# GpSimd takes over sums of squares and residual additions, and some weight splits are held back

## The reference, cut to what matters

```python
def rms_norm(x, w):
    xf = x.astype(jnp.float32)
    y = xf * lax.rsqrt(jnp.mean(xf * xf, -1, keepdims=True) + RMS_EPS)
    return (y * w.astype(jnp.float32)).astype(x.dtype)
...
    for i in range(DEPTH):                       # first block, DEPTH = 2
        a_in = rms_norm(hs, norm_w[i, 0])
        mix = gated_deltanet(a_in, ...) if i % N_MIXERS == 0 else mlstm(a_in, ...)
        hs = hs + keep * rms_norm(mix, norm_w[i, 1])                     # post-norm, residual
        f = conv_ffn(rms_norm(hs, norm_w[i, 2]), ffn_w_up[i], ..., ffn_w_down[i])
        hs = hs + keep * rms_norm(f, norm_w[i, 3])                       # post-norm, residual
...
    x = x + 0.5 * swiglu(rmsnorm(x, ffn1_norm), ffn1_w_gu, ffn1_w_down)  # second block
    z = rmsnorm(x, mix_norm) @ w_in
    ...
    x = x + merged @ w_out
    x = x + 0.5 * swiglu(rmsnorm(x, ffn2_norm), ffn2_w_gu, ffn2_w_down)
```

## Time and profile before

| | |
|---|---|
| median of 3 runs | 1910.94 us (1909.84 to 1913.47) |
| the profiled execution, its own time | 1910.32 us |
| its span | 1908.6 us |
| TensorE busy (matmul / weight load) | 1705.0 / 1614.5 us |
| VectorE, ScalarE, GpSimd busy | 1094.9, 832.7, 281.5 us |
| mean granted TensorE clock | 0.941 |

### The profile page before, as it was taken

One profiled execution on the slowest core, in us unless ns is written; L12 is line 12 of the kernel. 1 busy time (PEld: TensorE's weight loads), 2 busy tenths in 40 slices (PEclk: granted clock), 3 DMA queues, 4 the chain that ended last, 5 costly groups with the idle time before them and its releaser, 6 DMA issues.

```text
span 1908.6 us, 32571 instructions
## 1 busy us (share of the span) xinstructions
PE 1705.0 (89%) x13057; PEld 1614.5 (85%) x13057; DVE 1094.9 (57%) x1433; ACT 832.7 (44%) x1226; POOL 281.5 (15%) x343
## 2 busy tenths in 40 slices
PE   5986888889879999897579999799999989889998
PEld 4975888879869999795369999799998579889998
DVE  4862655556458864533458864555556376565654
ACT  5651233244446644542246654344443234644332
POOL 0000443410003320000003330122000000111120
PEclk8996799999989999895789999899999999999999
DMA  5540110115425444450025546354463343355543
GB/s 212 179 155 20 48 43 6 45 35 196 148 89 176 169 139 165 156 176 22 12 89 178 176 140 202 120 196 166 162 207 124 111 177 122 112 187 173 179 156 131
DMA packets 41566, 252.81 MB, mean 132 GB/s; under 512 B 4524, under 2 KB 6688, under 8 KB 19472
## 3 DMA queue, kind: packets, MB, share of 16 engines
q1 hardware_dynamic: 37376, 233.13, 35.7%
q0 software_dynamic: 4112, 18.61, 3.1%
HBM read 250.55 MB, written 1.17 MB: 132 GB/s over the span
## 4 chain that ended last, share of the span: by engine, by line
PE 77%; DVE 12%; ACT 6%; issue 3%; DMA 1%; POOL 1%; DVEq 0%; SPq 0%; ACTq 0%; POOLq 0%
PE bank L393 19%; PE bank L394 19%; PE bank L395 19%; ACT w_hi L281 3%; DVE w_lo L284 2%; PE bank L1088 2%; PE bank L397 2%; PE bank L563 2%; PE bank L1096 2%; PE bank L1099 2%; DVE rs L516 1%; PE bank L502 1%; DVE a L522 1%; DVE mix L522 1%; PE bank L1370 1%
## 5 line engine op out<-in xcount | busy, mean ns | idle before, releaser
L393 PE MATMUL bank<-work_r,w_hi 128*128 128x272 f32 (+1 forms) x3312 | 950.5, 287 | 63.3 <-DVE work_r L452 38.7
L394 PE MATMUL bank<-work_r,w_hi 128*128 128x272 f32 (+1 forms) x3312 | 944.3, 285 | 0.0
L395 PE MATMUL bank<-work_r,w_lo 128*128 128x272 f32 (+1 forms) x3312 | 943.5, 285 | 0.0
L284 DVE TENSOR_TENSOR w_lo<-ring,w_hi 128x2048 fp32r<-128x2048 f32 (+2 forms) x233 | 487.8, 2095 | 470.9 <-ACT w_hi L281 470.7
L393 PEld LDWEIGHTS bank<-work_r,w_hi 128*128 128x128 f32 x3312 | 632.1, 191 | 69.8 <-issue 38.2
L394 PEld LDWEIGHTS bank<-work_r,w_hi 128*128 128x128 f32 x3312 | 630.9, 190 | 0.4
L395 PEld LDWEIGHTS bank<-work_r,w_lo 128*128 128x128 f32 x3312 | 630.8, 190 | 0.0
L281 ACT ACTIVATE w_hi<-ring 128x2048 fp32r<-128x2048 f32 (+2 forms) x233 | 408.1, 1753 | 388.9 <-PE bank L395 388.8
L1248 DVE SCALAR_TENSOR_TENSOR work<-work,params_sb 128x272 f32<-128x272 f32 x176 | 122.7, 736 | 5.9
L1258 POOL TENSOR_TENSOR work<-work 128x272 f32<-128x272 f32 x44 | 44.9, 1020 | 344.6 <-ACT work L1232 344.6
L502 PE MATMUL bank<-sq,consts_sb 128*128 128x272 f32 (+1 forms) x170 | 48.7, 443 | 25.6 <-ACT sq L482 14.3
(11 more groups left out here) (387 smaller groups left out, 1881.7 us busy)
## 6 DMA issues: line engine op xcount, KB each, us to landing
ring<-in_stream SPq DMA_DIRECT2D x166, 1024.0 KB, 4.9
ring<-in_stream SPq DMA_DIRECT2D x64, 704.0 KB, 4.0
ring<-in_stream SPq DMA_DIRECT2D x10, 768.0 KB, 4.2
work<-rows_scratch POOLq DMA_DIRECT2D x4, 1632.0 KB, 8.0
work<-rows_scratch POOLq DMA_DIRECT2D x4, 544.0 KB, 9.1
work<-rows_scratch_o POOLq DMA_DIRECT2D x1, 2176.0 KB, 9.0
ring<-in_stream SPq DMA_DIRECT2D x3, 512.0 KB, 7.1
work<-rows_scratch_m POOLq DMA_DIRECT2D x1, 1088.0 KB, 7.1
```

What stands on the lines that cost most here:

```text
L284: eng.tensor_tensor(w_lo[:, slot, 0:size], raw_w, w_hi[:, slot, 0:size].bitcast(F32), ALU.subtract).then_inc(lo_done, 1)
L393: pe.matmul(out, w_hi[:, slot, at:at + P], hi, start=first, stop=False)
L394: pe.matmul(out, w_hi[:, slot, at:at + P], lo, start=False, stop=False)
L395: mm = pe.matmul(out, w_lo[:, slot, at:at + P], hi, start=False, stop=last)
```

## The change

Six sums of squares are shortened on TensorE: the four post-norms and the sums of in_uv and up3. GpSimd adds the squares of blocks 1 to 6 onto block 0 as they appear (`square_sums_pool`), and TensorE sums only that and block 7 (`norm_pooled_pe`). The residual additions of the four post-norms go from VectorE to GpSimd (`residual_pool`). At the four ends of the first block the split of the second slab of the next phase is held (`end="hold"`) and made by `prepare` later: on ScalarE behind the root of the post-norm, on VectorE behind the multiplications. ScalarE's square-root table is loaded at the start of the evacuations and not before the two roots that follow. `up2` has a lead of one slab where it had two; `up_dve` evacuates its first products before it splits, and in_uv's ScalarE splits before its first activation.

```diff
@@ each_product @@
+                body_first = split_last or begin == "body" and j == 0
+                if body_first:
                     body(Unit(ph, size, j, i, per_turn_))
-                if split:
+                if split and not (begin == "split" and per_turn_ == 0 and j == ph.parts - 1):
                     lo, hi = j * size * ph.per_product, (j + 1) * size * ph.per_product
                     slabs = range(lo // ph.parts, hi // ph.parts)
+                    if begin == "split" and j == 0:
+                        ahead(0, None)
                     for slab in slabs if end is None else slabs[:-1]:
                         ahead(slab, None if per_turn_ == 0 else i)
-                if not split_last:
+                if not body_first:
                     body(Unit(ph, size, j, i, per_turn_))
@@ new functions @@
+        def square_sums_pool(pool, turn, kind, use, n):
+            S.begin("square_sums")
+            for k in range(1, DB - 1):
+                pool.wait_ge(*S.at(f"{kind}_act", f"sq{k}", use))
+                if k > 1:
+                    S.own(pool, "square_sums", turn)
+                S.inc(pool.tensor_tensor(sq[:, 0, 0:n], sq[:, 0, 0:n], sq[:, k, 0:n], ALU.add), "square_sums")
+
+        def norm_pooled_pe(pe, turn, kind, use, n):
+            S.begin(f"{kind}_pe")
+            pe.wait_ge(*S.at("square_sums", turn=turn))
+            pe.matmul(stat[kind][:, 0:n], ones, sq[:, 0, 0:n], start=True, stop=False)
+            pe.wait_ge(*S.at(f"{kind}_act", f"sq{DB - 1}", use))
+            S.inc(pe.matmul(stat[kind][:, 0:n], ones, sq[:, DB - 1, 0:n], start=False, stop=True), f"{kind}_pe", "sums")
@@ norm_dve @@
-                if add is not None and 1 <= k <= blocks:
-                    dve.wait_ge(*S.at(f"{kind}_dve", f"k{k - 1}", use))
-                    S.inc(dve.tensor_tensor(add[1](k - 1), add[1](k - 1), dst(k - 1), ALU.add), "norm_add", k - 1)
+        def residual_pool(pool, use):
+            S.begin("norm_add")
+            for k in range(DB):
+                pool.wait_ge(*S.at("norm_dve", f"k{k}", use))
+                S.inc(pool.tensor_tensor(hs[:, k, :], hs[:, k, :], mix[:, k, :], ALU.add), "norm_add", k)
@@ evac_mix_act, up_act, up_dve, uv_act @@
-            each_product(act, name, 1, body, turns=0, split="hi", end="body")
+            act.preload_act_table(ACT.Sqrt)
+            each_product(act, name, 1, body, turns=0, split="hi", end="hold")
-            each_product(act, name, 2, body, ACT.Silu, split="hi")
+            each_product(act, name, 2, body, ACT.Silu, split="hi", lag=1)
-            each_product(dve, name, 2, body, split="lo", late=late, lag=1)
+            each_product(dve, name, 2, body, split="lo", late=late, lag=1, begin="body")
-            each_product(act, "in_uv", 1, body, turns=0, split="hi")
+            each_product(act, "in_uv", 1, body, turns=0, split="hi", begin="split")
@@ GpSimd's program @@
+            square_sums_pool(pool, 0, "norm", 1, T)
+            residual_pool(pool, 1)
             conv_up_pool(pool, 0)
+            square_sums_pool(pool, 1, "norm", 3, T)
+            residual_pool(pool, 3)
@@ ScalarE's program @@
-                norm_act(act, 1 + 4 * layer, None, 8, T, D)
-                norm_act(act, 2 + 4 * layer, H1, 8, T, D, ready=lambda k: act.wait_ge(*S.at("norm_add", k, 2 * layer)))
+                norm_act(act, 1 + 4 * layer, None, 8, T, D, table=False)
+                prepare(act, "hi", f"up{layer}")
+                norm_act(act, 2 + 4 * layer, H1, 8, T, D, ready=lambda k: act.wait_ge(*S.at("norm_add", k, 2 * layer)), table=False)
@@ VectorE's program @@
-                norm_dve(dve, 1 + 4 * layer, T, M1, gain("norm_w", (4 * layer + 1) * DB), M1, 8, add=(2 * layer, H1))
+                norm_dve(dve, 1 + 4 * layer, T, M1, gain("norm_w", (4 * layer + 1) * DB), M1, 8)
+                prepare(dve, "lo", f"up{layer}")
@@ TensorE's program @@
-                norm_pe(pe, 1 + 4 * layer, 8, T)
+                norm_pooled_pe(pe, 2 * layer, "norm", 1 + 4 * layer, T)
-            stream_pe(pe, "up2", a2_parts(7), SEQ, lead=2, after_block=lambda k: input_sum_pe(pe, 0, k))
+            stream_pe(pe, "up2", a2_parts(7), SEQ, lead=1, after_block=lambda k: input_sum_pe(pe, 0, k))
-            stream_pe(pe, "in_uv", in_x, SEQ, lead=1, after_lead=lambda: norm_pe(pe, 1, 8, SEQ, kind="pre"))
+            stream_pe(pe, "in_uv", in_x, SEQ, lead=1, after_lead=lambda: norm_pooled_pe(pe, 4, "pre", 1, SEQ))
```

More of the change, by code:

```diff
@@ L293, in each_product @@
         def each_product(eng, name, size, body, table=None, turns=None, split=None, late=None, lag=0, between=None,
-                         split_last=False, end=None):
+                         split_last=False, begin=None, end=None):
             ph = PLAN[name]
@@ L357, in each_product @@
                 unit(j, 0, 0, end if j == total - 1 else None)
-            for j in range(total - lag, total):
+            for j in range(total - lag if late is not None else total, total):
                 late(Unit(ph, size, j, 0, 0))
@@ L510, in input_sum_pe, with norm_dve @@
                 S.inc(mm, "pre_pe", "sums")
-        def norm_dve(dve, use, n, src, gain, dst, blocks, add=None, kind="norm", after=None):
+        def norm_dve(dve, use, n, src, gain, dst, blocks, kind="norm", after=None):
             S.begin(f"{kind}_dve")
@@ L517, in norm_dve @@
             dve.wait_ge(*S.at(f"{kind}_dve", "rstd", use))
-            if add is not None:
-                S.begin("norm_add")
-            for k in range(blocks + (1 if after is None else 2)):
+            for k in range(blocks + (0 if after is None else 2)):
                 if k < blocks:
@@ L2122, in _ @@
                 evac_mix_act(act, f"down{layer}", 3 + 4 * layer)
[L2123 to L2124 removed]
+                norm_act(act, 3 + 4 * layer, None, 8, T, D, table=False)
+                prepare(act, "hi", "up2" if layer else "ml_in")
             for k in range(DB):
@@ L2213, in _ @@
             split_dve(dve, 2, qkv[:, 16:32, :], O_HI, O_LO, 16, T)
-            each_product(dve, "gdn_out", 1, nothing, split="lo")
+            each_product(dve, "gdn_out", 1, nothing, turns=0, split="lo", end="hold")
             for layer in range(2):
@@ L2226, in _ @@
                     split_dve(dve, 5, hT, ML_HI, ML_LO, 8, T)
-                    each_product(dve, "ml_out", 1, nothing, split="lo")
+                    each_product(dve, "ml_out", 1, nothing, turns=0, split="lo", end="hold")
                 mix_was_read(dve, "gdn_out" if layer == 0 else "ml_out")
-                norm_dve(dve, 1 + 4 * layer, T, M1, gain("norm_w", (4 * layer + 1) * DB), M1, 8, add=(2 * layer, H1))
+                norm_dve(dve, 1 + 4 * layer, T, M1, gain("norm_w", (4 * layer + 1) * DB), M1, 8)
+                prepare(dve, "lo", f"up{layer}")
                 S.begin("ffn_zero")
@@ L2235, in _ @@
                 conv_up_dve(dve, layer)
-                each_product(dve, f"down{layer}", 1, nothing, split="lo")
+                each_product(dve, f"down{layer}", 1, nothing, turns=0, split="lo", end="hold")
                 mix_was_read(dve, f"down{layer}")
-                if layer:
-                    prepare(dve, "lo", "up2")
-                norm_dve(dve, 3 + 4 * layer, T, M1, gain("norm_w", (4 * layer + 3) * DB), M1, 8, add=(2 * layer + 1, H1),
+                norm_dve(dve, 3 + 4 * layer, T, M1, gain("norm_w", (4 * layer + 3) * DB), M1, 8,
                          after=(lambda k: input_dve(dve, k, 7, gain("ffn1_norm"))) if layer else None)
+                prepare(dve, "lo", "up2" if layer else "ml_in")
             input_scale_dve(dve, 0)
@@ L2361, in _ @@
             stream_pe(pe, "mix_out", split_input(pe, M_HI, M_LO, SEQ, by_step(pe, 9)), SEQ)
-            stream_pe(pe, "up3", a2_parts(10), SEQ, lead=1, after_lead=lambda: norm_pe(pe, 2, 8, SEQ, kind="pre"))
+            stream_pe(pe, "up3", a2_parts(10), SEQ, lead=1, after_lead=lambda: norm_pooled_pe(pe, 5, "pre", 2, SEQ))
             stream_pe(pe, "down3", hidden_input(pe, hid2_hi, hid2_lo, SEQ, "hid_pool", FB + 4), SEQ)
```

13 lines of the change are left out of this document (8 added, 5 removed).

## The result

| | before | after |
|---|---|---|
| median | 1910.99 us (4 runs, 1909.84 to 1913.47) | 1895.05 us (4 runs, 1890.91 to 1896.34) |
| the profiled execution, its own time | 1910.32 us | 1890.91 us |
| its span | 1908.6 us | 1888.8 us |

The ratio of after to before is 0.9911, 95% interval 0.9892 to 0.993: 17.0 us, between 13.4 and 20.6. The two medians lie 15.9 us apart. Forecast was 1894.

A forecast was written before the change was run, and what follows sets the result against it. TensorE, 77% of the chain that ended last, was taken as the bound. -0.6 + 9.35 + 4.5 + 3.7 = 17.0 us off 1910.32 gives 1893.3, median 0.6 above: 1894 us, range 1889 to 1899, with near rivals 1886 to 1903.

The forecast's parts named there:

- First root: At four post-norms: split and table load leave the root's path and sums shrink to two records; reciprocal 3.15 us earlier.
- Double norms: Behind gdn_out, down0 and ml_out: VectorE and GpSimd take turns, the eighth addition waits for the split; 0.2 us lost each.
- The rival without exclusion: At the three double norms: residual additions 2.1 us faster each, 6.3 us in all, giving 1888 us; chance 12%.
- The new table load at the start of the evacuations costs nothing: At the four post-norms: ScalarE has nothing to evacuate for the length of a product, so the early load is free.
- up2: At up2's start: TensorE begins 2.8 us earlier and the 6.52 us stall before the third slab is filled; gain 9.35 us.
- in_uv and up3: At both starts: twelve of sixteen sum records go, and the stalls of 1.74 and 0.96 us; gains 4.5 and 3.7 us.
- Sum: Whole kernel: -0.6 + 9.35 + 4.5 + 3.7 = 17.0 us gained.
- The rival in which up2 fills only in part: At up2's start: TensorE waits for blocks and stays at the lower clock; gain 11 us, giving 1900 us; chance 16%.
- 1.46: At four places, rival: GpSimd's additions become the bound; at 1.46 us each the 17 us gain is gone; chance 8%.

The follow-up runs named there:

- the held split made late: The changed kernel with VectorE's held split moved behind the split of the next phase's input at the three double norms: 1887.57 us, ratio to before 0.9864.
- the three ends alone: The kernel before with the change at the ends of gdn_out, down0 and ml_out only: 1912.18 us, ratio to before 0.9997.
- the late load: The changed kernel with the square-root table loaded behind the first evacuation of a down or out product: 1892.33 us, ratio to before 0.9877.
- the kernel with both edits: The changed kernel with additions back on VectorE and its held split behind the input's split: 1885.82 us, ratio to before 0.9859; again 1889.26 us, 0.9856.

## Why the prediction was right, and where it was not

**First root.** Forecast 3.15 us earlier, with the reciprocal 1.6 us behind the products. It is 1.9 (535.45 behind an end of 533.58), so 2.9 earlier. The two-record sums stand at all six places, 12 records at L514 and 12 at L516. One reading was wrong and cost nothing: GpSimd's additions of squares were put at 0.77 to 1.07 us each. Their median is 1.92, since most stand beside a split of VectorE, and they come in time only because the products are further apart (duration min/median/max in ns):

```profile
L508 POOL TENSOR_TENSOR sq<-sq x36: 735/1921/2599, 499.6 to 1703.1; 128x272 f32<-128x272 f32 x24, 128x256 f32<-128x256 f32 x12
```

**Double norms.** Forecast a pair of 0.93, an eighth addition of about 2.7 and a loss of 0.2 us in each; measured 0.92, 2.80, and 14.79 against 14.58, so 0.2, at gdn_out, and the same at down0 and ml_out. The rival without exclusion is refuted by the held split made late and by the three ends alone. At the next phase's fourth split the loss is 0.8 behind down0 and ml_out, since TensorE's first records stand in a longer stretch of low clock there (behind down0 from 778.07 to 784.0, 5.9 us; before, from 776.57 to 781.3, 4.7 us); the forecast had no term for that.

**"The new table load at the start of the evacuations costs nothing, since ScalarE has nothing to evacuate for the length of a product."** This step failed. ScalarE had nothing to evacuate but had the third slab to split, and TensorE waits for that split at the starts of down0 and down1. It cost 2.0 and 0.4 us in the profiled execution; the late load took it away.

**up2.** Forecast 9.35 us, measured 12.1. The mechanism held to within a few tenths: start 2.6 earlier (with down1's shift taken off), no stall, the third split ready 17.2 us behind TensorE's start, where 17.5 was forecast. At the fourth split the gain was 10.54 - 1.01 = 9.5. The term left out is the 2.55 between the fourth and the ninth split, the low clock behind the old stall. It stood in the forecast only as a spread of the clock, not as part of the stall's price. The cost of a block in the lead, forecast at 1.3 us, was 1.32.

**in_uv and up3.** Forecast 4.5 and 3.7, measured 4.9 and 3.4.

**Sum.** Forecast 17.0; by the ledger 16.2, and by the times 17.0. The low clock at up2 (+2.6) and the table load with the longer low stretches (-2.4 and -1.2) nearly cancel: that the total is righter than its terms is luck. The rival in which up2 fills only in part didn't come about: TensorE had no pause in its lead. Its price was worked out too low: 11.8 us of work at full clock take 11.8 more at half, not 6, so that rival stood for about 1906 and not 1900. GpSimd's additions had a median of 0.955, far below 1.46.

## What to carry to other kernels

Price a stall of TensorE with the clock behind it: here 6.52 us of waiting cost 9, since a stretch at half clock followed. Elementwise work with two SBUF inputs that was moved from VectorE to GpSimd didn't run beside VectorE's work of the same kind here but in turns with it, and a long instruction queued behind it on VectorE held up the last short one on GpSimd until it was nearly done: 2.04 us were gone by queueing the split later. And before an instruction is put into a gap of an engine, look at what that engine does for the weights there, not only for the results.

## What the runs showed of the hardware

**The spacing of matmuls isn't the same in each execution, at the same granted clock.** Neighbouring matmuls of 256 columns start either 113.3 or 117.8 ns apart, for a whole phase, at a granted clock of 1.00 and with TensorE busy throughout. The same program shows both: a window of up3 in the first and in the second profile of the kernel with both edits.

```profile
1730.00:1800.00 70.00, 70.00 (x620) 70.00 (x619) 42.01 (x51) 30.28 (x26) 14.86 (x26) 1.00 0.56 190
```

```profile
1730.00:1800.00 70.00, 70.00 (x597) 70.00 (x596) 40.08 (x49) 29.51 (x25) 14.35 (x25) 1.00 0.55 192
```

620 against 597 records in the same 70 us, 3.9%. Over up3 that is near 4 us. up3 was at the slow spacing in the profile of before and at the fast one in that of after, which is the 3.8 us of the ledger's last row; up3 was at the fast spacing, too, in the kernel with three ends only, whose up3 is that of before, so the spacing isn't the change's. up2 took either too, and phases of 272 columns showed 123.3 or 126.7 ns. What chooses isn't known. It explains part of why one program's times spread over 11 to 18 us, and it means that a difference between two profiles should be booked by place: what grows evenly over a long phase isn't the change's.

**Whether the clock falls behind a short wait differs too.** The same two waits of 0.8 and 1.55 us were followed by a low clock at down0 in both profiles of the change, at down1 in one of them. Over all profiles the double wait stands at 13 starts of down0 or down1, and the clock fell behind it at 11, for about 3.4 us each time. The single wait of 2.16 to 2.18 us stands at 13 others, and the clock fell at one, the down0 shown above. What decides it isn't known.
